# Layer norms of a two-layer backbone: the variance moved from VectorE's statistics operations to a squaring pass on ScalarE

## The chip, the cores and the metric

The kernel runs on one core of a Trainium2 chip. The metric is the device time of one execution in microseconds (us): the median of three runs of the kernel before is 2028.66 us, and its runs lie between 2025.94 and 2029.03 us. TensorE does matmuls and transposes, VectorE and ScalarE do elementwise work, GpSimd does a little elementwise work and starts some of the DMAs, and SyncE starts the weight DMAs.

## The reference, cut to what matters

Two layers of a backbone work on 384 tokens (128 context tokens and 256 latent ones) of width 1024. Each layer has three sub-layers (feed-forward, token mixer, feed-forward), and each ends in a layer norm of a weighted sum:

```python
def layer_norm(x, g, b):
    mu = jnp.mean(xf, -1, keepdims=True)
    var = jnp.mean(jnp.square(xf - mu), -1, keepdims=True)
    return ((xf - mu) * lax.rsqrt(var + LN_EPS) * g + b).astype(x.dtype)
...
    h = x * (1.0 + sc1) + sh1
    f = swiglu(h, lp['ffn_w_gate'][0], lp['ffn_w_up'][0], lp['ffn_w_down'][0])
    x = layer_norm(ALPHA * x + 0.5 * g1 * f, lp['ln_g'][0], lp['ln_b'][0])
```

So there are six norms in one execution. The output of a norm, modulated by a scale and a shift, is the input of the next sub-layer. The last norm gives the result.

## The kernel before, in words

The 384 tokens are three groups `g` of 128, one token per partition, in the tile `x[:, g, :]` (128 x 1024 float32). Norm `n` (0 to 5) stands behind sub-layer `n`. Norms 0 to 4 are worked in `turn_x(j)` of each engine's program, the lead-in of the next sub-layer, which has number `t = n + 1`, and `j = t % 3` (1: into a mixer; 0 or 2: into a feed-forward part); norm 5 is `norm_last`. Each engine runs its own instructions in program order, and the order across engines is made by semaphores alone, all written by hand. What an engine does for a group in a norm, in order of dependence:

- TensorE finishes the group's accumulation (`acc_done`).
- VectorE `residual(n, g)`, L2167: two products of 512 columns, from PSUM times the gate, into a residual tile. It frees the accumulation banks (`acc_read`).
- VectorE `rest(n, g)`, L2175: `x = ALPHA * x + residual` (L2178), two `bn_stats` of 512 columns (L2180), one `bn_aggr` that gives mean and variance (L2182, `stats_ready`).
- ScalarE `root(n, g)`, L1652: the square root of variance plus epsilon (L1654, `std_ready`).
- VectorE `scale(n, g)`, L2184: the reciprocal (L2186), and the mean times it, negated (L2187, `rstd_ready`).
- ScalarE `normalise(n, g)`, L1657: `x = x * rstd - mean * rstd` (L1659, `normed`).
- TensorE `turn_group(t, g)`, L826: eight transposes into two PSUM banks (`turned`).
- ScalarE `modulate`, L1664, on the first half and VectorE `modulate`, L2196, on the second half: scale and shift of the next sub-layer.
- ScalarE `high`, L1674: the rounded part of the modulated tile; VectorE `low`, L2206: the rest to it (`h_ready`). TensorE multiplies both, so its first product of the next sub-layer waits for `low` of group 0 and for the first half of `low` of group 1.

`weight(u)` is the same split of a unit of weights: ScalarE rounds it (L1650), VectorE takes the rest (L2161). The next sub-layer begins with groups 0 and 1 together in `tile_first` (L959), and takes group 2 behind them. In `turn_x` of VectorE for t of 2 and more (L2253 to L2276) the order is residual, rest and scale of group 0, the same of group 1, modulation of 0, residual of 2, weight 0, modulation of 1, the three `low` operations, weight 1, then rest and scale of group 2. ScalarE's order (L1713 to L1772) has the modulation of group 0 ahead of the root of group 1 for j of 2, and behind its normalisation for j of 0 and 1; for j of 0 two weights stand between normalisation 0 and root 1. For t of 1 VectorE takes all three groups one after the other (L2237), and ScalarE's queue has `ride_copy` and `ride_out` between them, copies of small products that SyncE's weight chunks and GpSimd's table of shifts (`ab_ready`) depend on. TensorE runs a few products without use (`keep_clock`, L837) while it waits.

In `norm_last` (L2329) VectorE does residual, rest and `finish` of one group after the other, and `finish` (L2332) applies gain and bias in two three-operand operations, in halves for the last group, whose stores follow.

## Time and profile before

| what | value |
|---|---|
| median of three runs | 2028.66 us (2025.94 to 2029.03) |
| span of the profiled execution | 2027.0 us |
| TensorE matmul busy | 1918.1 us, 95% |
| VectorE busy | 1042.7 us, 51% |
| ScalarE busy | 703.9 us, 35% |
| mean granted TensorE clock | 0.973 of full |

The span goes from the first to the last instruction of the profiled execution; it lies 1.66 us below the median of the timed runs and inside their range. A busy share is an average over stages. What a norm is worth is read from the stretch around it, by what each engine waits for there. In the rows, PE is TensorE, DVE is VectorE, ACT is ScalarE, L2180 is line 2180 of the kernel before, and a bracket at the end of a row gives the idle time in front of the instruction and what ended it.

### The profile page before, as it was taken

The numbers are of one execution on the slowest core, as the hardware profiler recorded it, in microseconds if no ns is written. First come the engines' busy times: TensorE is split into PE (matmuls) and PEld (weight loads), VectorE is DVE, ScalarE is ACT, GpSimd is POOL, SyncE is SP. The second block draws the span as 40 slices with busy tenths as digits, with TensorE's granted clock in tenths as the row PEclk, the third lists the DMA queues.
The fourth block names the chain that finished last, engine by engine and source line by source line (L and its number), as shares of the span: only waits on it lengthen the run. The fifth ranks groups of instructions, "written<-read, shape, count | busy, mean of one in ns | idle before, by whom it ended". The sixth has DMA issues, their size and how long they took to land.

```text
span 2027.0 us, 37395 instructions
## 1 busy us (share of the span) xinstructions
PE 1918.1 (95%) x16214; PEld 1731.7 (85%) x16214; DVE 1042.7 (51%) x1653; ACT 703.9 (35%) x1170; POOL 33.7 (2%) x69
## 2 busy tenths in 40 slices
PE   6999999998899899999999999999987989999996
PEld 5899997987679779999979999989766877899996
DVE  2333336555565775333364333466557768533336
ACT  3222224444442353222252222245364224322221
POOL 0000000000000001000000000000000000000000
PEclk8999999999989999999999999999998899899998
DMA  8733336333680145333344333323344004333330
GB/s 325 296 124 124 124 127 247 104 125 125 248 335 18 42 151 189 124 124 124 125 166 145 124 124 124 131 77 125 104 176 171 4 24 162 111 124 124 124 104 32
DMA packets 41473, 277.71 MB, mean 137 GB/s; under 512 B 4778, under 2 KB 6810, under 8 KB 9344
## 3 DMA queue, kind: packets, MB, share of 16 engines
q1 hardware_dynamic: 35424, 255.34, 34.9%
q0 software_dynamic: 3312, 16.91, 2.2%
q10 hardware_dynamic: 2608, 3.56, 0.5%
q8 instruction: 104, 1.70, 0.3%
q14 instruction: 25, 0.20, 0.0%
HBM read 269.22 MB, written 3.41 MB: 134 GB/s over the span
## 4 chain that ended last, share of the span: by engine, by line
PE 81%; DVE 11%; ACT 3%; issue 2%; DMA 1%; PEld 0%; ACTq 0%; PEldq 0%; SPq 0%; POOL 0%; DVEq 0%; POOLq 0%
PE bank L919 17%; PE bank L984 17%; PE bank L923 17%; PE bank L922 17%; PE bank L759 2%; PE bank L1372 1%; DMA ring<-weights 1%; PE bank L1361 1%; PE bank L1379 1%; DVE ring_r L2161 1%; DVE ln_stat L2180 1%; DVE x L2178 1%; PE bank L840 1%; PE bank L768 1%; DVE arena L2171 1%
## 5 line engine op out<-in xcount | busy, mean ns | idle before, releaser
L2161 DVE TENSOR_TENSOR ring_r<-ring,arena_r 128x1024 fp32r<-128x1024 f32 x328 | 387.7, 1221 | 706.5 <-ACT arena_r L1650 706.0
L919 PE MATMUL bank<-arena_r 128*128 128x384 f32 (+3 forms) x2056 | 700.8, 341 | 13.3 <-DVE arena_r L2210 11.2
L923 PE MATMUL bank<-arena_r,ring_r 128*128 128x384 f32 (+2 forms) x1816 | 604.9, 333 | 0.0
L922 PE MATMUL bank<-arena_r 128*128 128x384 f32 (+2 forms) x1816 | 602.9, 332 | 0.0
L919 PEld LDWEIGHTS bank<-arena_r 128*128 128x128 f32 x2056 | 391.5, 190 | 35.5 <-issue 20.0
L1650 ACT ACTIVATE arena_r<-ring 128x1024 fp32r<-128x1024 f32 x340 | 340.4, 1051 | 138.0 <-PE bank L923 136.6
L922 PEld LDWEIGHTS bank<-arena_r 128*128 128x128 f32 x1816 | 343.5, 189 | 3.5
L923 PEld LDWEIGHTS bank<-arena_r,ring_r 128*128 128x128 f32 x1816 | 343.6, 189 | 0.0
L984 PE MATMUL bank<-arena_r 128*128 128x512 f32 x1128 | 310.9, 393 | 0.3 <-issue 0.3
L1781 ACT ACTIVATE arena<-bank 128x384 f32<-128x384 f32 x88 | 43.3, 492 | 740.5 <-PE bank L923 740.5
L984 PEld LDWEIGHTS bank<-arena_r 128*128 128x128 f32 x1128 | 210.7, 188 | 42.2 <-issue 1.2
L984 PE MATMUL bank<-ring_r,arena_r 128*128 128x512 f32 x456 | 142.0, 392 | 0.0
L984 PEld LDWEIGHTS bank<-ring_r,arena_r 128*128 128x128 f32 x456 | 85.6, 188 | 19.8
L923 PE MATMUL bank<-arena_r 128*128 128x512 f32 (+1 forms) x240 | 89.7, 374 | 0.0
L922 PE MATMUL bank<-ring_r,arena_r 128*128 128x512 f32 (+1 forms) x240 | 89.4, 373 | 0.0
L759 PE MATMUL bank<-ring,silu_c 128*32 128x256 f32 x1152 | 73.6, 396 | 15.3 <-DMA const<-consts 9.6
L759 PEld LDWEIGHTS bank<-ring,silu_c 128*32 128x32 f32 x1152 | 34.8, 112 | 43.1 <-issue 18.9
L2297 DVE TENSOR_TENSOR arena<-arena,bank 128x384 f32<-128x384 f32 x88 | 48.2, 547 | 29.4 <-PE bank L923 29.4
L922 PEld LDWEIGHTS bank<-ring_r,arena_r 128*128 128x128 f32 x240 | 45.6, 190 | 9.6 <-issue 1.9
L923 PEld LDWEIGHTS bank<-arena_r 128*128 128x128 f32 x240 | 45.5, 189 | 8.5
L785 ACT ACTIVATE ride_row<-bank 112x512 f32<-112x512 f32 x36 | 21.4, 594 | 87.4 <-PE bank L759 87.3
L2301 DVE TENSOR_TENSOR arena_r<-arena,arena_r 128x384 fp32r<-128x384 f32 x88 | 49.2, 559 | 3.1
(295 smaller groups left out, 1817.6 us busy)
## 6 DMA issues: line engine op xcount, KB each, us to landing
ring<-weights SPq DMA_DIRECT2D x242, 1024.0 KB, 4.9
lnrow<-ln_in POOLq DMA_DIRECT2D x6, 1024.0 KB, 6.8
const<-consts POOLq DMA_DIRECT2D x1, 2211.0 KB, 9.5
arena<-gate POOLq DMA_DIRECT2D x4, 385.0 KB, 8.0
x<-x_in ACTq DMA_DIRECT2D x1, 1536.0 KB, 13.7
rows<-row_in POOLq DMA_DIRECT2D x2, 704.0 KB, 10.7
par<-par_in POOLq DMA_DIRECT2D x2, 662.5 KB, 7.5
y_out<-x SPq DMA_DIRECT2D x2, 512.0 KB, 2.6
```

The lines of the kernel that those rows point to most:

```text
L759: mm = pe.matmul(ps[bank][rows_at, half * 256:half * 256 + 256], silu_c[:, 2 * (k % 2):2 * (k % 2) + 32], ring_tile(n + half)[:, k, :], st ...
L768: mm = pe.matmul(ps[bank][:, at + 2 * i:at + 2 * i + 2], ride_row[:, number % 2, i * P:i * P + P], sel, start=True, stop=True)
L785: sc.activation(ride_row[0:RIDE_ROWS, number % 2, :], ps[bank][0:RIDE_ROWS, :], ACT.Copy).then_inc(ride_copied, 1)
L919: mm = pe.matmul(out, w_h, h_h, start=start, stop=False, skip_group_check=True)
L922: pe.matmul(out, w_h, h_l, start=False, stop=False, skip_group_check=True)
L923: return pe.matmul(out, w_l, h_h, start=False, stop=stop, skip_group_check=True)
L984: mm = pe.matmul(ps[2 + 2 * g + n][:, :], a[:, tok], w[:, n * 512:n * 512 + 512], start=(first and a is a_hi and w is hi), stop=(last and ...
L1650: sc.activation(place, unit_of((l, name), u), ACT.Copy).then_inc(w_rounded, 1)
L1781: sc.activation(sgt[:, b, :], ps[0][:, 0:TOK], ACT.Silu).then_inc(silu_done, 1)
L2161: ve.tensor_tensor(low_unit((l, name), u) if out is None else out, raw, place.bitcast(F32), ALU.subtract).then_inc(w_ready, 1)
L2297: ve.tensor_tensor(act[:, b, :], sgt[:, b, :], ps[1][:, 0:TOK], ALU.mult).then_inc(act_ready, 1)
L2301: ve.tensor_tensor(lo, act[:, b, :], hi.bitcast(F32), ALU.subtract).then_inc(act_split, 1)
```

## The change

The three statistics operations of `rest` go. The residual operation (L2178) gets an accumulator output, the row sum; one operation of one column turns it into the negated mean. `root` on ScalarE squares `x` minus the mean over all 1024 columns with a row sum, its output going to the spent residual tile, waits for it, and takes the root of the sum over 1024 plus epsilon. `scale` multiplies the negated mean by the reciprocal. VectorE's order in `turn_x` changes: `residual` of the next group stands ahead of `scale` of a group, `scale` of group 1 goes behind `modulate` of group 0, `rest` of group 2 goes ahead of the three `low` operations and its `scale` behind them, ahead of weight 1. The case t = 1 is written out in the same manner. ScalarE's order stays. In `norm_last` the product with the gain is taken before the root is there, into a tile of its own, and one operation (for the last group one of each half) is left behind the reciprocal.

```diff
--- before.py
+++ after.py
@@ -315,7 +315,6 @@
         ride_row = sb("ride_row", [P, 2, 512])
         gate = sb("gate", [P, 2, DM])
         lnrow, lnrow_r = with_rounded("lnrow", [P, 2, DM])
-        ln_stat = sb("ln_stat", [P, GROUPS, 12])
         small = sb("small", [P, 216])
         arena, arena_r = with_rounded("arena", [P, 23704])
 
@@ -528,7 +527,7 @@
         bonus = small[:, 136:160]
         gla_end_decay = small[:, 160:162]
         first_bias = small[:, 192:216]
-        ln_mv = small[:, 177:183].rearrange("p (g n) -> p g n", g=GROUPS)
+        ln_mean = small[:, 177:183].rearrange("p (g n) -> p g n", g=GROUPS)
         ln_r = small[:, 183:192].rearrange("p (g n) -> p g n", g=GROUPS)
         diff_gn = lnrow[:, 1, 0:P]
         eps_col = small[:, 176:177]
@@ -1650,8 +1649,11 @@
                         sc.activation(place, unit_of((l, name), u), ACT.Copy).then_inc(w_rounded, 1)
 
                     def root(n, g):
+                        spent = res_mix[:, g, :] if n % NMIX == 1 else res_ffn[:, g % 2, :]
                         sc.wait_ge(stats_ready, GROUPS * n + g + 1)
-                        sc.activation(ln_r[:, g, 0:1], ln_mv[:, g, 1:2], ACT.Sqrt,
+                        own.link(sc.activation(spent, x[:, g, :], ACT.Square, bias=ln_mean[:, g, 1:2],
+                                               accum_out=ln_r[:, g, 0:1]))
+                        sc.activation(ln_r[:, g, 0:1], ln_r[:, g, 0:1], ACT.Sqrt, scale=1.0 / DM,
                                       bias=eps_col[:, 0:1]).then_inc(std_ready, 1)
 
                     def normalise(n, g):
@@ -2175,21 +2177,16 @@
                     def rest(n, g):
                         res = res_of(n, g)
                         ve.wait_ge(acc_read, GROUPS * n + g + 1)
-                        own.link(ve.scalar_tensor_tensor(x[:, g, :], x[:, g, :], ALPHA, res, ALU.mult, ALU.add))
-                        for i in range(2):
-                            own.step(ve.bn_stats(ln_stat[:, g, 6 * i:6 * i + 6], x[:, g, i * 512:i * 512 + 512]))
-                        own.settle()
-                        ve.bn_aggr(ln_mv[:, g, :], ln_stat[:, g, :]).then_inc(stats_ready, 1)
+                        own.link(ve.scalar_tensor_tensor(x[:, g, :], x[:, g, :], ALPHA, res, ALU.mult, ALU.add,
+                                                         accum_out=ln_mean[:, g, 0:1]))
+                        ve.tensor_scalar(ln_mean[:, g, 1:2], ln_mean[:, g, 0:1], -1.0 / DM, None,
+                                         ALU.mult).then_inc(stats_ready, 1)
 
                     def scale(n, g):
                         ve.wait_ge(std_ready, GROUPS * n + g + 1)
                         own.link(ve.reciprocal(ln_r[:, g, 1:2], ln_r[:, g, 0:1]))
-                        ve.scalar_tensor_tensor(ln_r[:, g, 2:3], ln_mv[:, g, 0:1], -1.0, ln_r[:, g, 1:2], ALU.mult,
-                                                ALU.mult).then_inc(rstd_ready, 1)
-
-                    def statistics(n, g):
-                        residual(n, g)
-                        rest(n, g)
+                        ve.tensor_tensor(ln_r[:, g, 2:3], ln_mean[:, g, 1:2], ln_r[:, g, 1:2],
+                                         ALU.mult).then_inc(rstd_ready, 1)
 
                     LOWER, UPPER = slice(0, 4), slice(4, KT)
 
@@ -2235,9 +2232,15 @@
 
                         n = t - 1
                         if t == 1:
-                            for g in range(GROUPS):
-                                statistics(n, g)
-                                scale(n, g)
+                            residual(n, 0)
+                            rest(n, 0)
+                            residual(n, 1)
+                            scale(n, 0)
+                            rest(n, 1)
+                            residual(n, 2)
+                            scale(n, 1)
+                            rest(n, 2)
+                            scale(n, 2)
                             ve.wait_ge(ab_ready, t + 1)
                             modulate(j, 0)
                             modulate(j, 1)
@@ -2252,22 +2255,24 @@
                             return
                         if j == 1:
                             weight(0)
-                        statistics(n, 0)
+                        residual(n, 0)
+                        rest(n, 0)
+                        residual(n, 1)
                         scale(n, 0)
-                        statistics(n, 1)
-                        scale(n, 1)
+                        rest(n, 1)
                         ve.wait_ge(ab_ready, t + 1)
                         modulate(j, 0)
+                        scale(n, 1)
                         residual(n, 2)
                         if j != 1:
                             weight(0)
                         modulate(j, 1)
+                        rest(n, 2)
                         low(j, 0, 0)
                         low(j, 1, 1, LOWER)
                         low(j, 2, 1, UPPER)
+                        scale(n, 2)
                         weight(1)
-                        rest(n, 2)
-                        scale(n, 2)
                         if j != 1:
                             for u in range(2, 4):
                                 weight(u)
@@ -2328,15 +2333,17 @@
 
                     def norm_last():
                         n = NMIX * DEPTH - 1
+                        gained = arena[:, 0:GROUPS * DM].rearrange("p (g n) -> p g n", g=GROUPS)
 
                         def finish(g):
 
+                            ve.wait_ge(stats_ready, GROUPS * n + g + 1)
+                            own.step(ve.scalar_tensor_tensor(gained[:, g, :], x[:, g, :], ln_mean[:, g, 1:2], lnrow[:, 0, :],
+                                                             ALU.add, ALU.mult))
                             ve.wait_ge(std_ready, GROUPS * n + g + 1)
                             own.link(ve.reciprocal(ln_r[:, g, 1:2], ln_r[:, g, 0:1]))
                             for c in (slice(0, 512), slice(512, DM)) if g == GROUPS - 1 else (slice(0, DM),):
-                                own.link(ve.scalar_tensor_tensor(x[:, g, c], x[:, g, c], ln_mv[:, g, 0:1], lnrow[:, 0, c],
-                                                                 ALU.subtract, ALU.mult))
-                                ve.scalar_tensor_tensor(x[:, g, c], x[:, g, c], ln_r[:, g, 1:2], lnrow[:, 1, c], ALU.mult,
+                                ve.scalar_tensor_tensor(x[:, g, c], gained[:, g, c], ln_r[:, g, 1:2], lnrow[:, 1, c], ALU.mult,
                                                         ALU.add).then_inc(x_ready, 1)
 
                         ve.wait_ge(lnrow_loaded, 16 * NMIX * DEPTH)
```

## Rows read from the trace of the kernel before

**Rows 1.** the page: the span, and the chain that ended last by engine

```profile
span 2027.0 us, 37395 instructions
...
PE 81%; DVE 11%; ACT 3%; issue 2%; DMA 1%; PEld 0%; ACTq 0%; PEldq 0%; SPq 0%; POOL 0%; DVEq 0%; POOLq 0%
```

**Rows 2.** instructions by line and shape, VectorE; columns: count | busy us, mean ns | idle before

```profile
L2180 DVE BATCH_NORM_STATS2 ln_stat<-x 128x6 f32<-128x512 f32 x36 | 23.2, 685 | 0.6
...
L2178 DVE SCALAR_TENSOR_TENSOR x<-x,arena 128x1024 f32<-128x1024 f32 x18 | 22.0, 1223 | 0.5
...
L2182 DVE BATCH_NORM_AGGREGATE small<-ln_stat 128x2 f32<-128x12 f32 x18 | 3.8, 209 | 0.6
```

**Rows 3.** the same view, ScalarE: normalisation, root, its table load, read-out of a row sum

```profile
L1659 ACT ACTIVATE x<-x,small 128x1024 f32<-128x1024 f32 x15 | 18.7, 1244 | 6.4 <-DVE small L2187 6.4
...
L1654 ACT ACTIVATE small<-small 128x1 f32<-128x1 f32 x18 | 5.3, 294 | 79.3 <-DVE small L2182 79.3
...
L1654 ACT ACT_TABLE_LOAD x4 | 5.1, 1283 | 0.1
...
L1926 ACT ACTIVATION_READ_ACCUMULATOR wad<-arena 128x1 f32 x24 | 4.8, 201 | 0.0
```

**Rows 4.** timeline of ScalarE in layer 0's mixer; columns: start us, us, line, operation

```profile
698.41 1.49 ACT L2103 ACTIVATE arena<-arena 128x1536 f32<-128x1536 f32 x1 [1.48 <-DVE arena L2784]
...
702.45 1.28 ACT L2110 ACT_TABLE_LOAD   x1
```

**Rows 5.** the chain that ended last, final norm; columns: start us, us, what

```profile
2009.87 1.21 DVE arena L2171 x2
...
2017.06 1.21 DVE arena L2171 x2
...
2023.88 0.75 DVE x L2339
```

**Rows 6.** timeline, norm 1 (behind layer 0's mixer): up to the first products

```profile
735.54 1.50 ACT L1670 ACTIVATE arena<-bank,ab 128x128 f32<-128x128 f32 x4
...
740.10 1.06 PE L834 MATMUL bank<-const,x 128*128 128x128 f32 x8 [0.29 <-issue]
...
741.67 1.36 DVE L2202 TENSOR_SCALAR arena<-bank,ab 128x128 f32<-128x128 f32 x4
...
742.95 2.42 DVE L2210 TENSOR_TENSOR arena_r<-arena,arena_r 128x1024 fp32r<-128x1024 f32 x3
...
744.91 0.36 PE L919 MATMUL bank<-arena_r 128*128 128x256 f32 x1 [1.51 <-DVE arena_r L2210]
```

**Rows 7.** timeline, norm 1: the third group of 128 tokens

```profile
754.45 1.36 DVE L2202 TENSOR_SCALAR arena<-bank,ab 128x128 f32<-128x128 f32 x4
...
756.55 0.30 PE L919 MATMUL bank<-arena_r 128*128 128x128 f32 x1 [1.38 <-DVE arena_r L2210]
```

**Rows 8.** timeline, norm 2 (behind layer 0's second feed-forward part)

```profile
1028.25 1.99 ACT L1650 ACTIVATE arena_r<-ring 128x1024 fp32r<-128x1024 f32 x2
...
1033.38 1.06 PE L834 MATMUL bank<-const,x 128*128 128x128 f32 x8 [0.29 <-ACT x L1659]
...
1039.03 0.36 PE L919 MATMUL bank<-arena_r 128*128 128x256 f32 x1 [1.65 <-DVE arena_r L2210]
```

**Rows 9.** timeline, norm 3 (behind layer 1's first feed-forward part)

```profile
1328.70 1.96 PE L903 MATMUL bank<-arena,wad 128*64 128x128 f32 x16 [2.01 <-ACT arena L1670]
...
1333.02 2.42 DVE L2210 TENSOR_TENSOR arena_r<-arena,arena_r 128x1024 fp32r<-128x1024 f32 x3
...
1341.41 1.06 PE L834 MATMUL bank<-const,x 128*128 128x128 f32 x8 [0.29 <-ACT x L1659]
```

**Rows 10.** timeline, norm 0: root of the third group

```profile
338.97 0.28 ACT L1654 ACTIVATE small<-small 128x1 f32<-128x1 f32 x1
```

**Rows 11.** stretches: length, busy us (instructions) of each engine, granted clock, DMA share, GB/s

```profile
1325.00:1350.00 25.00, 20.94 (x162) 19.53 (x161) 14.22 (x36) 11.32 (x22) 0.00 (x0) 0.93 0.00 1
1720.00:1760.00 40.00, 38.25 (x208) 35.22 (x209) 24.32 (x33) 15.47 (x24) 0.54 (x1) 0.87 0.32 120
```

## The prediction

> **What bounds the kernel now.** I read the page first: the chain that ended last is TensorE for 81% of the span and VectorE for 11% [rows 1]. So inside a sub-layer VectorE and ScalarE cost nothing, and a norm counts only where TensorE waits for it. Then I went through the timeline around each of the six norms, looking on TensorE's rows for a bracket. At norms 0 to 4 TensorE stands before the first product of the next sub-layer (1.51 and 1.65 us at norms 1 and 2 [rows 6, 8]) and again before the third group (1.38 us [rows 7]). Behind norm 5 no matmul is left: the chain is VectorE alone, 7.19 us from one group to the next (2009.87 to 2017.06), and 7.57 us from there to the last operation's end (2023.88 + 0.75) [rows 5]. In the lead-in of norm 1 VectorE is busy without a break from 741.67 to the first product; in that of norm 2 ScalarE's queue carries the start (two weights at 1028.25, the normalisation, then transposes at 1033.38) [rows 6, 8].
>
> **The change, one group alone.** Removed from VectorE: two statistics of 0.685 us and one closing operation of 0.209; back to back with their gaps they fill 1.56 us of the path. Kept: the residual operation, 1.223 us [rows 2]. Added on VectorE: the read of the row sum and an operation of one column. No VectorE row shows an accumulator output; the nearest is ScalarE's read, 0.201 us [rows 3]. It may hide wholly, so I bound it by 0 and 0.20 and take 0.10, between. The one-column operation is bounded by the closing operation it resembles, 0.21 [rows 2], and I take 0.20 with its gap. Added on ScalarE: the square over 1024 columns. With two column operands such an ACTIVATE takes 1.244 [rows 3], with none about 1.0 (1.99 for two [rows 8]); it has one, so 1.15, and its read adds 0.10 of its 0.20 behind it (bounds 0 and 0.20). New path: 0.30 + 0.03 + 1.25 = 1.58 against 1.56. **The latency of one group doesn't change.** VectorE gets 1.26 us free, ScalarE gets 1.25 more. The change is worth something only where VectorE is the bound and has other work meanwhile.
>
> **The table load.** The root needs ScalarE's table to be changed behind each feed-forward part: four loads of 1.283 us, with 0.1 us of idle in front of all four together [rows 3]. Today they are issued while the engine would wait for statistics (79.3 us of waiting ahead of the 18 roots [rows 3]), at no cost. In the mixer a square stands ahead of a root: the square at 698.41 has no load in front of it, the load comes at 702.45, directly ahead of the root [rows 4]. I take it that the same happens here: the square runs under the old table and the load comes between square and root. It then lies on the first group's path at norms 0, 2, 3 and 5, at 1.28 us each.
>
> The Trainium skill's page "ScalarE: Activation LUTs", section "Table sets: the hidden batching unit", says that cheap functions are in every set as filler and that the load is placed right before the activation whose function is not in the active set. By that rule, which speaks against this change, the load comes behind the square; the mixer's rows agree for one set, and no row here shows a square under the feed-forward part's set. If it were not there, the third rival below holds.
>
> **Norm 5** (nothing hides it). Group 0: latency 1.56 is traded for 1.58, the gain product (1.28) runs beside the square, and the load adds 1.28: 0.0. Group 1: the gain product leaves the path: 7.19 - 1.28 = 5.9, -1.3. Group 2: the two halves' gain products leave, 1.5: -1.5. Sum -2.8, bounds -3.1 and -2.3 by the reads.
>
> **Norms 1 and 4** (behind a mixer, twice the same). ScalarE modulates group 0 from 735.54 for 1.50 [rows 6], to 737.04, and only then comes to root 1, although VectorE's sum for group 1 is ready some 2.5 us sooner than the statistics were. Square and read 1.25, root 0.29 [rows 3], VectorE's two small operations 0.36, normalisation 1.24 [rows 3], less one overlap: 740.2, and the transposes start at 740.35 instead of 740.10 [rows 6]. Their second half is there 1.1 later, at 741.45; VectorE modulates 1.36, to 742.8, a little ahead of before (741.67 + 1.36 [rows 6]). But now `rest` of group 2 stands ahead of the three `low` operations: 1.22 + 0.30 = 1.53, to 744.35. From the start of the `low` operations to the first product were 744.91 - 742.95 = 1.96 [rows 6]: first product at 746.3, +1.4. At the third group VectorE's modulation began at 754.45 only when weights 2 and 3 were done [rows 7]; group 2's root is now earlier and they will be out of the way. ScalarE's half limits that: -0.5, bounds 0 and -1.0, inside the 1.38 of waiting there [rows 7]. **+0.9 each.** Weight 1 now waits behind `scale` of group 2, and so behind a square; it comes just in time for the second early product (2.9 us behind the first); if not, up to +0.4.
>
> **Norm 2.** VectorE's latency being equal, ScalarE is later by the load: its two weights end at 1028.25 + 1.28 + 1.99 = 1031.5 [rows 8]. Square and read 1.25, root 0.29, small operations 0.40, normalisation 1.24: 1034.7, transposes from 1033.38 to 1034.95, +1.6 [rows 8]. Second half 1.1 later, modulation 1.36, `rest` of group 2 1.53, 1.96 to the first product: 1040.9 instead of 1039.03 [rows 8], +1.9. Weight 1 is late here by 0.3, the third group gives back 0.5: **+1.7**.
>
> **Norm 3.** TensorE is still at work on the last tiles, which hides the load. But `scale` of group 1 now waits behind `modulate` of group 0, and the square is on ScalarE: modulation 0 and the first `features` product (1328.70 with 2.01 of waiting [rows 9]) come 1.2 later. The `low` operations, at 1333.02 before [rows 9], come 1.2 + 1.53 later. Before, TensorE took the first product at about 1335.2, 0.2 behind them because of its own work; so +2.5. The third group's transposes at 1341.41 waited 0.29 for a normalisation [rows 9], which is early now: **+2.2**.
>
> **Norm 0.** The root of group 2 at 338.97 [rows 10] stands on the path by ScalarE's queue: its statistics were long there. Behind it are the copies that the table of shifts waits for. So the square is added whole, 1.25, and the scale of group 1, now behind the residual of group 2, delays a copy by up to 0.4. **+1.6.**
>
> **Sum:** 1.6 + 0.9 + 1.7 + 2.2 + 0.9 - 2.8 = +4.5. Against the profiled span that is 2027.0 + 4.5 = 2031.5; that execution's span lies 1.66 below the median of the runs, so 2033.2. A tile inside a feed-forward part is bound by TensorE, so what is lost ahead of it isn't regained. What a measurement can tell from no change is about 0.2%, 4.1 us: the bounds are 2024.6 and 2032.7.
>
> **Rivals.**
> 1. A further clock fall. In the lead-in of norm 4 the granted clock falls: 0.87 over 40 us [rows 11], so 0.13 x 2 x 40 = 10.4 us at the lower level, 1.2 instead of 2.4 GHz, which costs half of it, 5.2. Norms 1 and 2 have nearly the same waits and their rows no fall. The change makes TensorE's wait ahead of norm 1's first product 2.7 instead of 1.5. One more such fall: 2033.2 + 5 = 2038.
> 2. The other side, not slower: the clock is regained. If the wait at the third group, shorter by 0.5, no longer ends in a fall at norm 4, -5.2; the smaller fall at norm 3 (0.93 over 25 us [rows 11], 3.5 us at the lower level) gives 1.8 at most. It decides from one fall gone: 2028.0; with both, 2026.2; with both and the lead-ins half as dear, 2023. Against it: other waits grow.
> 3. The load goes ahead of the square, hidden as before: -1.3 at norm 5 and -1.3 at norm 2, none at norms 0 and 3: 2030.6.
> 4. The lead-ins are hidden and only norm 5 counts: 2028.7 - 2.8 = 2025.9; with the load hidden too, 2024.6. For it: 1.26 us less of VectorE per group where VectorE is the bound. Against it: ScalarE's order, and the place of `rest` of group 2.
> 5. The change doesn't do what it says (the sum is not kept by the operation and the pass is rebuilt): within 0.2%.
>
> **How the numbers follow.** Forecast 0.38, of it 0.31 slower and 0.07 same (its own range, 2031 to 2035.5, crosses the bound); rival 1 0.18, slower; rival 2 0.21, 0.13 same and 0.08 faster; rival 3 0.08, same; rival 4 0.12, 0.08 same and 0.04 faster; rival 5 0.03, same. Slower 0.49, same 0.39, faster 0.12. The likeliest is the forecast, 2033.2. Range 2025.5 to 2038.5: it takes in rivals 3 and 5, most of 1, 2 and 4, and leaves out some 0.08 below and 0.08 above.
>
> **What would show it.** Per group: the row sum ready 1.55 us behind the residual product, a square of 1.15. A table load between the first square and root of norms 0, 2, 3 and 5; if it stands ahead of the square, that step is wrong. First product behind the transposes: 1.4 later at norm 1, with the sum operation of group 2 between VectorE's modulation and `low`. The end: 5.9 us from group 1 to group 2. The prediction is wrong if the accumulator costs far more than 0.2 on VectorE, if the lead-ins don't lengthen, or if stretches at the lower clock appear or vanish.

## The result: 0.59% slower, and the profile after

| | before | changed |
|---|---|---|
| median of 7 runs | 2028.66 us | 2037.03 us |
| lowest and highest | 2020.76 to 2032.96 | 2035.55 to 2039.71 |
| profiled execution, span | 2027.0 | 2033.4 |

The ratio of the two kernels is 1.0059, with a 95% interval of 1.0042 to 1.0076: 12 us slower, between 8.5 and 15.4. (It isn't the quotient of the medians, which lie 8.4 us apart.) The sign was forecast, the size was not: +4.5 lies below the whole interval. The page of the changed kernel, span and chain that ended last (before: [rows 1]):

```profile
span 2033.4 us, 37412 instructions
...
PE 84%; DVE 8%; ACT 4%; issue 2%; DMA 1%; PEld 0%; ACTq 0%; PEldq 0%; SPq 0%; DVEq 0%; POOL 0%; POOLq 0%
```

VectorE's share of the chain fell from 11 to 8%, ScalarE's rose from 3 to 4%, and TensorE's rose from 81 to 84%, although it has the same matmuls to do. That last figure is the trail to follow.

Instructions of the changed kernel by line and shape (line, engine, operation, count | busy us, mean ns | idle before); they answer to [rows 2, 3]:

```profile
L2180 DVE SCALAR_TENSOR_TENSOR x<-x,arena 128x1024 f32<-128x1024 f32 x18 | 22.0, 1221 | 0.3
...
L1654 ACT ACTIVATE arena<-x,small 128x1024 f32<-128x1024 f32 x18 | 20.7, 1148 | 48.9 <-DVE small L2182 48.9
...
L1661 ACT ACTIVATE x<-x,small 128x1024 f32<-128x1024 f32 x15 | 18.6, 1242 | 13.6 <-DVE small L2188 13.6
...
L1656 ACT ACT_TABLE_LOAD x4 | 5.1, 1283 | 0.1
...
L1654 ACT ACTIVATION_READ_ACCUMULATOR arena<-x,small 128x1 f32 x18 | 3.4, 190 | 0.0
```

The square takes 1.148 us where 1.15 was taken. The residual operation, now with a row sum, takes the 1.22 us it took without one.

**Norm 5**, the chain that ended last in the changed kernel (start us, us, what); it answers to [rows 5], to which this row of the kernel before, the start of its group 0, belongs:

```profile
2002.59 1.30 DVE arena L2171 x2
```

The changed kernel:

```profile
2012.08 1.30 DVE arena L2173 x2
...
2014.68 0.16 DVE small L2182
...
2014.87 1.24 ACT arena L1654 x2
...
2016.13 1.28 ACT L1656
...
2019.23 1.21 DVE arena L2173 x2
...
2025.01 1.21 DVE arena L2173 x2
...
2029.49 0.75 DVE x L2346
2030.24 0.66 DVEq L802
```

From group 0 to group 1 it takes 7.15 us (7.28 before), from group 1 to group 2 5.78 (7.19 before), and from there to the end of the last operation 5.89 (7.57 before). The load of 1.28 us lies on the path at 2016.13, behind the square. Norm 5 got 3.2 us shorter.

**Norm 1**, timeline of the changed kernel (start us, us, engine, line, operation, in brackets the wait ahead and who ended it); it answers to [rows 6]:

```profile
743.55 1.07 PE L833 MATMUL bank<-const,x 128*128 128x128 f32 x8 [0.50 <-ACT x L1661]
...
744.65 1.37 DVE L2199 TENSOR_SCALAR arena<-bank,ab 128x128 f32<-128x128 f32 x4 [0.20 <-PE bank L833]
...
745.94 1.22 DVE L2180 SCALAR_TENSOR_TENSOR x<-x,arena 128x1024 f32<-128x1024 f32 x1
...
747.08 0.08 DVE L2180 DVE_READ_ACCUMULATOR x<-x,arena 128x1 f32 x1
...
747.27 2.42 DVE L2207 TENSOR_TENSOR arena_r<-arena,arena_r 128x1024 fp32r<-128x1024 f32 x3
...
749.23 0.35 PE L918 MATMUL bank<-arena_r 128*128 128x256 f32 x1 [2.38 <-DVE arena_r L2207]
```

Group 2's sum stands between modulation and `low`, as forecast, and costs 1.33 (745.94 to 747.27). Modulation follows the transposes in 1.10 instead of 1.57 (741.67 - 740.10 [rows 6]); before, VectorE was at the rest of a weight until then, and now it is free sooner. The read of the row sum takes 0.08 us and the residual operation ends under it.

**Norm 2**, timeline of ScalarE in the changed kernel:

```profile
1031.43 1.15 ACT L1654 ACTIVATE arena<-x,small 128x1024 f32<-128x1024 f32 x1 [9.70 <-DVE small L2182]
1032.49 0.18 ACT L1654 ACTIVATION_READ_ACCUMULATOR arena<-x,small 128x1 f32 x1
1032.69 1.28 ACT L1656 ACT_TABLE_LOAD   x1
1033.98 0.29 ACT L1656 ACTIVATE small<-small 128x1 f32<-128x1 f32 x1
```

The square runs under the table of the feed-forward part, and the load comes behind it, directly ahead of the root.

**The clock.** A fall, below, is a stretch in which the granted clock is the lower of its two levels, 1.2 instead of 2.4 GHz. Stretches over the lead-ins of norms 0, 1, 2, 3 and 4 in the changed kernel (length, busy us of each engine, granted clock, DMA share, GB/s), and then over norms 0, 1 and 2 in the kernel before:

```profile
330.00:365.00 35.00, 32.01 (x272) 28.00 (x271) 14.64 (x36) 18.29 (x38) 1.14 (x5) 0.95 0.48 191
735.00:765.00 30.00, 25.44 (x203) 20.14 (x202) 18.07 (x37) 21.57 (x37) 0.00 (x0) 0.94 0.45 176
1028.00:1064.00 36.00, 31.59 (x229) 25.32 (x228) 21.15 (x42) 24.66 (x40) 0.00 (x0) 0.95 0.47 176
1310.00:1355.00 45.00, 40.53 (x246) 37.44 (x245) 23.46 (x44) 20.91 (x31) 0.00 (x0) 0.96 0.27 94
1715.00:1760.00 45.00, 40.45 (x289) 34.33 (x288) 29.99 (x52) 28.44 (x46) 0.00 (x0) 0.96 0.39 152
```

```profile
325.00:362.00 37.00, 34.52 (x318) 29.19 (x316) 20.70 (x44) 17.18 (x35) 1.14 (x5) 1.00 0.57 233
730.00:760.00 30.00, 25.95 (x213) 20.31 (x212) 23.35 (x43) 19.01 (x32) 0.00 (x0) 1.00 0.46 176
1022.00:1055.00 33.00, 29.52 (x226) 23.31 (x225) 24.91 (x45) 19.78 (x33) 0.00 (x0) 1.00 0.49 192
```

Each of the five lead-ins now has one short stretch of 3.4 us at 1.2 GHz (0.05 x 2 x 35 = 3.5), where before norms 0, 1 and 2 had none. In exchange the longer fall at norm 4 (0.87 over 40 us [rows 11]) is gone from this execution.

**The feed-forward parts.** Nothing in the change touches them, and still each takes longer at full clock. In the chain that ended last the down products of a tile appear once per tile, as one row. (A feed-forward part is the stretch of a feed-forward sub-layer between two lead-ins; there are four, 0 to 3.) The 1st and the 16th of these rows in part 0, kernel before, then changed kernel:

```profile
105.52 4.17 PE bank L984 x18
...
294.28 4.15 PE bank L984 x18
```

```profile
105.75 4.17 PE bank L983 x18
...
295.25 4.17 PE bank L983 x18
```

15 tiles in 188.76 us against 189.50: a tile takes 12.584 us before and 12.633 after. There are 88 tiles, so some 4 us. No step of the prediction has this.

To see what each stretch costs, I set the matmuls of two traces beside each other one for one (the small ones that keep the clock left out) and took the time between the same two. Where no fall of the clock lies in a feed-forward part, these times repeat from one execution to the next within some 0.05 us. "low" is the time at 1.2 GHz, "from" the start of the stretch in the kernel before:

| stretch, us | from | before | changed |
|---|---|---|---|
| start | 0 | 87.52 (low 10.2) | 87.65 (low 10.2) |
| ffn part 0 | 87.52 | 238.53 | 239.50 |
| norm 0 lead-in | 326.05 | 34.75 | 37.18 (low 3.4) |
| mixer 0 | 360.79 | 368.44 (low 30.7) | 368.23 (low 23.9) |
| norm 1 lead-in | 729.23 | 29.12 | 31.15 (low 3.4) |
| ffn part 1 | 758.36 | 250.43 | 251.44 |
| norm 2 lead-in | 1008.79 | 44.15 | 46.62 (low 3.4) |
| ffn part 2 | 1052.94 | 243.68 | 244.63 |
| norm 3 lead-in | 1296.61 | 52.98 (low 3.4) | 54.86 (low 3.4) |
| mixer 1 | 1349.60 | 333.67 (low 41.0) | 332.97 (low 34.1) |
| norm 4 lead-in | 1683.27 | 55.34 (low 5.4) | 55.09 (low 3.4) |
| ffn part 3 | 1738.61 | 258.54 (low 4.9) | 257.33 |
| norm 5 and end | 1997.15 | 29.89 | 26.71 |

### The profile page after: what moved, and what is told of

Its sections match the earlier page's. It is cut to its first block, busy times and chain, and to the rows that moved or that the text cites. A ratio compares the mean times of both kernels' runs of the same rounds, so it can differ in the third digit from the quotient of the medians.

```text
span 2033.4 us, 37412 instructions
## 1 busy us (share of the span) xinstructions
PE 1921.4 (94%) x16214; PEld 1731.9 (85%) x16214; DVE 1019.6 (50%) x1634; ACT 724.3 (36%) x1206; POOL 33.7 (2%) x69
## 4 chain that ended last, share of the span: by engine, by line
PE 84%; DVE 8%; ACT 4%; issue 2%; DMA 1%; PEld 0%; ACTq 0%; PEldq 0%; SPq 0%; DVEq 0%; POOL 0%; POOLq 0%
PE bank L918 18%; PE bank L921 17%; PE bank L922 17%; PE bank L983 17%; PE bank L758 2%; PE bank L1371 1%; DMA ring<-weights 1%; PE bank L1360 1%; PE bank L1378 1%; PE bank L839 1%; PE bank L767 1%; ACT arena L1672 1%; PE bank L833 1%; DVE x L2180 1%; ACT arena L1654 1%
```

## Experiments

Two theories stood at the start. **Place**: the change takes away a tile (`ln_stat`, 144 bytes of each partition), so `small` and the `arena`, which holds TensorE's operands, lie 144 bytes lower, and the matmuls run at another pitch. **Norms**: the lead-ins cost more than forecast, by themselves or by falls of the clock. Each series of timed kernels below was run beside the kernel before on one chip; its median there was 2025 to 2027 us. A mean clock or a time is of all timed executions of a kernel; stretches are of the one that was profiled. "Tiles in place" means the changed kernel with the unused tile of the second experiment.

### The kernel before again

No edit.

> The kernel before once more, profiled on the chip of the next three. It is the yardstick for two things: the pitch of the matmuls inside the feed-forward loops and the stretches at the lower TensorE clock. If the pitch belongs to the kernel, matmuls 600 to 1600 of TensorE take 190.5 us here as in the first profile (191.3 in the changed kernel). If it belongs to the chip or the execution, it is anything between. Ratio to itself 1.000.

Measured: ratio 0.9995 (0.9982 to 1.0009). So a difference under 0.2% says nothing here.

### Changed kernel, tiles back in place

```diff
+        spacer = sb("spacer", [P, GROUPS, 12])
         small = sb("small", [P, 216])
```

> The changed kernel with a tile of 144 bytes per partition put back where the statistics tile was, so that all later tiles lie where they lay before. Theory P (the place of the tiles sets the matmuls' pitch): the drift inside the four feed-forward parts, some 0.8 to 1.1 us in each and about 4 us in all, goes: about 4 us faster than the changed kernel, ratio to the kernel before 1.004. Theory Q (pitch is of the chip or execution): no difference to the changed kernel, ratio 1.006.

Measured: 2031.63 us, ratio 1.0021 (1.0007 to 1.0036). The feed-forward parts are 238.56, 250.44, 243.68 and 256.29 us, those of the kernel before (256.27 for the last, in an execution without a fall there). By the two ratios an unused tile takes back more than half of the loss.

### Kernel before, tiles moved

```diff
-        ln_stat = sb("ln_stat", [P, GROUPS, 12])
         small = sb("small", [P, 216])
         arena, arena_r = with_rounded("arena", [P, 23704])
+        ln_stat = sb("ln_stat", [P, GROUPS, 12])
```

> The kernel before with the same statistics tile allocated behind the large one, so that the large one and the small one lie 144 bytes lower, as in the changed kernel; no instruction differs. Theory P: about 4 us slower, ratio 1.002. Theory Q: ratio 1.000.

Measured: 2035.22 us, ratio 1.0054 (1.0034 to 1.0075), with not one instruction changed. Its chain that ended last, the same two tiles as above:

```profile
105.59 4.17 PE bank L984 x18
...
295.09 4.17 PE bank L984 x18
```

189.50 us, exactly the changed kernel's. So place alone makes a slower kernel, and the norms alone do not explain the result. Every product of a tile is made of three lines of matmuls (high by high, high by low, low by high). In part 0 the matmuls of 384 columns of the first line stand 175.9 ns ahead of the next one in the kernel before, and 179.4 here (means of 298); the two other lines move by 1.1 at most.

### Table load ahead of the wait

Edit on top of the changed kernel with its tiles in place:

```diff
+                        if g == 0 and n % NMIX != 1:
+                            sc.activation(table_col, eps_col, ACT.Sqrt)
                         sc.wait_ge(stats_ready, GROUPS * n + g + 1)
```

> The padded changed kernel with one more root of a single column ahead of the wait for group 0's sum at norms 0, 2, 3 and 5, so that the table load comes there. Forecast's step: 1.3 us less at norm 5 and 1.3 at norm 2, none at norms 0 and 3, so 2.6 us under e2. Rival (the load is covered by other work): no difference to e2.

Measured: ratio 1.0028 (1.0014 to 1.0042); the same, within the intervals, as without the edit. Norm 5 took 25.42 us instead of 26.68, the whole load. But norm 2's lead-in gained 0.3 only (45.19 instead of 45.46 at full clock). Timeline of norm 2 in this kernel, ScalarE and VectorE:

```profile
1031.78 0.30 ACT L1659 ACTIVATE small<-small 128x1 f32<-128x1 f32 x1
1031.81 1.29 DVE L2176 TENSOR_TENSOR arena<-bank,gate 128x512 f32<-128x512 f32 x2 [1.34 <-PE bank L984]
1033.01 0.15 DVE L2190 RECIPROCAL small<-small 128x1 f32<-128x1 f32 x1
...
1033.40 1.25 ACT L1664 ACTIVATE x<-x,small 128x1024 f32<-128x1024 f32 x1 [1.32 <-DVE small L2191]
```

The root ends at 1032.08, but its reciprocal stands behind the residual product of group 1, which VectorE took up at 1031.81, and ScalarE waits 1.32 us. What the early load gives, the new order on VectorE takes. So at norm 2 the load was not the price; order and load cover each other.

### Group 2's sum back in its old place

Edit on top of the changed kernel with its tiles in place: `rest(n, 2)` and `scale(n, 2)` behind the `low` operations and `weight(1)`, as before.

```diff
                         modulate(j, 1)
-                        rest(n, 2)
                         low(j, 0, 0)
...
+                        weight(1)
+                        rest(n, 2)
                         scale(n, 2)
-                        weight(1)
```

> The padded changed kernel with the sum operation of group 2 and its scale put back behind the three low operations and weight 1. The forecast's step: 1.5 us less ahead of the first product at norms 1, 2 and 4 and up to 2 at norm 3, so 5 us under e2, and the 0.5 us at the third group lost again where the weights 2 and 3 are late. Rival (ScalarE's queue is the bound, not this operation): under 1 us.

Measured: ratio 1.0039 (1.0020 to 1.0057), no gain. Norm 1 in this kernel:

```profile
745.35 1.37 DVE L2200 TENSOR_SCALAR arena<-bank,ab 128x128 f32<-128x128 f32 x4 [0.20 <-PE bank L834]
746.63 2.42 DVE L2208 TENSOR_TENSOR arena_r<-arena,arena_r 128x1024 fp32r<-128x1024 f32 x3
748.60 0.36 PE L919 MATMUL bank<-arena_r 128*128 128x256 f32 x1 [1.05 <-DVE arena_r L2208]
```

From modulation to first product it is 3.25 us instead of 4.58 (744.65 to 749.23), the 1.33 of the sum, as forecast. But then the third group is late by 1.0 of it, and the lead-in as a whole gains 0.34 (29.31 against 29.65). At norm 2 it gains nothing (45.44 against 45.46): VectorE still waits 1.31 us there for ScalarE's high parts, ahead of the second `low`, so the sum had cover. Norm 3 gains 0.9 (53.97 against 54.86, each with a fall of 3.4 us).

### New form at norm 5 alone

Norms 0 to 4 stay with `bn_stats` and their old order; norm 5 takes the new sum, square and `finish`, with the table load ahead of its wait; `ln_stat` stays, so the tiles are in place.

```diff
-                            root(n, g)
+                            square_root(n, g)
...
-                            rest(n, g)
+                            summed(n, g)
```

> The kernel before at norms 0 to 4, with the changed form at norm 5 alone and the table load ahead of the wait; all tiles lie where they lay before. Forecast's step: 4.1 us faster than before (0.0 + 1.3 for the load at group 0, 1.3, 1.5), ratio 0.998, with no change at any lead-in.

Measured: 2021.06 us, ratio 0.9979 (0.9961 to 0.9997). Norm 5 takes 25.43 us instead of 29.89, and nothing else moves. Again in a later series:

> The kernel with the new form at the last norm alone and the table load ahead of its wait, with its tiles as before, once more beside the others of this series: ratio 0.998 (2021 us where the kernel before takes 2025.5), which is the 4.5 us by which its last norm is shorter. The label's name notwithstanding, its arena is where it was before. It bounds how far a repeat of five rounds moves, and says whether the last norm's gain holds in a second series.

Measured: 2022.80 us, ratio 0.9978 (0.9964 to 0.9992). The 4.5 us hold.

### More matmuls to keep the clock

Edit on top of the changed kernel with its tiles in place:

```diff
-WARM_START, WARM_MIX, WARM_TURN, WARM_GLA = 22, 6, (3, 6, 10), (7, 10)
+WARM_START, WARM_MIX, WARM_TURN, WARM_GLA = 22, 10, (7, 8, 14), (7, 10)
```

> The padded changed kernel with four more products without use in each wait of TensorE at norms 1 to 4 (0.25 us each; two at norm 3's second wait). If the longer waits bring the short falls of the clock (one of 3.4 us in each lead-in of the changed kernel's profile, 1.7 us each), they go at norms 1 to 4 and up to 6 us come back; if the falls come at any rate, nothing does or up to 1 us is lost.

Measured: 2027.58 us, ratio 1.0007 (0.9991 to 1.0023), against 1.0021 (1.0007 to 1.0036) without the edit; the intervals overlap. The mean clock of the timed runs is 0.9796, against 0.9763. The profiled execution has one short fall, at norm 0, and two of 10 us in parts 1 and 2. That count alone says little: the kernel with group 2's sum back in its old place, without the added matmuls, has no short fall at norms 0, 1, 2 and 4.

Several executions with tiles in place give each lead-in at full clock (us): norm 0 36.18 (from the kernel with its tiles in place and the one with group 2's sum back in its place), norm 1 29.64, norm 2 45.46, norm 3 53.15, norm 4 53.65 (from this one). The kernel before has 34.75, 29.12, 44.15, 51.2 and 53.14; 51.2 is from kernels with the arena moved, which read 51.2 to 51.4, and 53.14 from the kernel with the new form at norm 5 alone.

### Changed kernel again, beside the others

No edit.

> The changed kernel unaltered, timed beside the kernel before in the same series as the others. If the place of the tiles costs what the shifted kernel before showed (some 1.0 us in each feed-forward part, about 4.4 us in all), this run lies about 4 to 6 us above the changed kernel with its tiles put back: ratio 1.004 to 1.006, with feed-forward parts at 239.5, 251.4, 244.6 and 257.3 us. If the place costs nothing in timed runs, the ratio is the 1.002 of the kernel with its tiles put back, and the rest of the 1.006 measured first belonged to that series.

Measured: 2037.15 us, ratio 1.0060 (1.0039 to 1.0081), with parts of 239.51, 251.43, 244.58 and 257.32 us. The 1.006 belongs to the kernel, not to its first series.

### Which bytes, and by what rule

Five places of the kernel before. The first was timed, the others were profiled once each. 4 unused bytes ahead of the arena (`spacer`, [P, 1]):

> The kernel before with the large tile moved up by 4 bytes, so that its start, 4 bytes short of a multiple of 64 bytes before and 20 bytes short in the changed kernel, is a multiple of 64. No instruction differs. If the pitch goes by how far operands lie from such a multiple, the 1.0 us per feed-forward part that 144 bytes down cost come with another sign or size: up to 16 ns of each product of 384 columns (175 ns now, 160 at 2.4 GHz), 80 us in all, at the most. If only a conflict between two tiles counts (distances inside the large tile don't change), the pitch stays as before: ratio 1.000.

Measured: ratio 1.0030 (1.0009 to 1.0051). 64 bytes ahead of it ([P, 16]):

> The kernel before with an unused tile of 64 bytes ahead of the operand arena: arena starts 64 bytes higher, its start modulo 64 stays 60. If the start modulo 64 sets the pitch of the feed-forward matmuls, the four parts take what they take before, 238.5, 250.4, 243.7 and 256.3 us. If it goes by another property of the address (modulo 128 or more, or the distance to another tile), they move by up to 1.0 us each. Timed runs are not asked for: without falls of the clock these parts repeat to 0.02 us.

16 bytes ([P, 4]):

> The kernel before with an unused tile of 16 bytes ahead of the arena: start modulo 64 is 12 in place of 60. If the pitch goes by the start modulo 64, the parts lie anywhere between 238.5 and 239.5 us for the first and move together, as with the 4 bytes (239.0). If only the distance to the small tiles below counts, they stay at 238.5.

`ln_stat` behind the arena and 16 bytes ahead of it, so the arena lies 128 bytes lower:

> The kernel before with the norm statistics' tile behind the arena and 16 bytes unused ahead of the arena: the small tiles lie 144 bytes lower, as in the changed kernel, the arena 128 bytes lower and so at its old start modulo 64. If the arena's start modulo 64 sets the pitch, the feed-forward parts are those of the kernel before (238.5, 250.4, 243.7, 256.3 us). If the place of the small tiles does, they are those of the changed kernel (239.5, 251.4, 244.6, 257.3 us).

And `ln_stat` behind the arena with 144 bytes ahead of it, so that only `small` is moved:

> The kernel before with the norm statistics' tile behind the arena and 144 unused bytes ahead of the arena: only the small tiles are moved, the arena starts at its old place. If the place of the arena alone sets the pitch of the matmuls, all parts are those of the kernel before: 238.5, 250.4, 243.7, 256.3 us. If the small tiles have a part in it, or the distance between the two, they differ by 0.3 us or more each.

Measured, feed-forward parts without falls of the clock, us (a dash where one lay in the part; the row of -144 is the changed kernel's, and parts 0, 1 and 3 of the moved one agree within 0.02). The last two columns are the heads of the mixers, between the same two matmuls in every trace (360.79 to 476.07 and 1349.60 to 1462.48 in the kernel before), where no execution has a fall:

| arena moved by | small moved by | part 0 | part 1 | part 2 | part 3 | mixer 0, head | mixer 1, head |
|---|---|---|---|---|---|---|---|
| 0 | 0 | 238.5 | 250.4 | 243.7 | 256.3 | 115.3 | 112.9 |
| 0 | -144 | 238.6 | 250.4 | 243.7 | - | 115.3 | 112.9 |
| -144 | -144 | 239.5 | 251.4 | 244.6 | 257.3 | 115.3 or 115.7 | 112.9 or 114.2 |
| +4 | 0 | 239.0 | 251.0 | 244.2 | 256.8 | 116.3 | 113.9 |
| +16 | 0 | 239.0 | 251.0 | 244.2 | - | 116.3 | 113.9 |
| +64 | 0 | 238.2 | - | 243.4 | 255.9 | 117.1 | 114.7 |
| -128 | -144 | 236.4 | 248.2 | 241.4 | 253.9 | 116.2 | 113.7 |

Of the two tiles it is the arena's place that counts: with only `small` moved nothing changes. And my rule fell: +64 and -128 leave the start modulo 64 as it was, and the first moves part 0 by 0.3 us and the second by 2.2.

The heads of the mixers move as well, and not by the same rule as the parts: +1.7 us in all at -128, where the parts are shortest, +2.0 at +4 and +16, and +3.7 at +64, more than the parts give back there. At -144 the place doesn't settle them: the changed kernel's first profiled execution has the heads of the kernel before, its second one and that of the moved kernel have 1.7 us more. So the place at -128 is worth -9.0 + 1.7 = -7.3 us, and the one at -144 +4.0 or +5.7. The tile's time at -128, from the chain of that kernel:

```profile
104.81 4.12 PE bank L985 x18
...
291.81 4.12 PE bank L985 x18
```

187.00 us for 15 tiles, 12.467 each, and every row of down products 0.03 to 0.05 shorter. In part 0 there, the three lines of matmuls stand 173.9, 173.5 and 174.0 ns ahead of the next one, steadily from the seventh matmul of a tile on. In the kernel before, the gaps go round in a pattern of nine matmuls, whose longest is 178 to 179 in one tile and 185 in the next; at -144 they go round in a pattern of six with one of 185 in every tile. So what differs is a rhythm in the starts of the matmuls. By what rule the place sets it stays open.

### Do place and norms add up?

The kernel before and the changed kernel, both with the arena 128 bytes lower, timed:

> The same kernel as the last one, timed. Its parts without falls of the clock sum to 9 us less than before: 2017 to 2019 us, ratio 0.995 to 0.997 to the kernel before. If that execution was an odd one, 1.000.

> The changed kernel with 16 unused bytes ahead of the arena, so that its tiles lie as in the last kernel (small tiles 144 bytes lower than before, arena 128 bytes lower). If the place of the tiles and the layer norms are two separate terms, the feed-forward parts are those of that kernel (236.4, 248.2, 241.4, 253.9 us), the layer norms those of the changed kernel, and the time lies some 13 us below the changed kernel and 3 to 7 us above the kernel before with the same tiles. If the short feed-forward parts came from something else in that one execution, they come back to 238 to 240 us.

Measured: 2021.41 us, ratio 0.9979 (0.9961 to 0.9996), and 2023.11 us, ratio 0.9984 (0.9968 to 1.0000). The changed kernel's parts are 236.4, 248.1, 241.4 and 253.9 us, its lead-ins those it has elsewhere. One unused tile of 16 bytes makes the changed kernel 14 us faster (2037.15 to 2023.11, in two series), and no slower than the kernel before.

The kernel before gained less in its timed runs (4 to 5 us) than its four parts give (9.0), and the moved kernel lost more (11) than its parts give (4.0). 1.7 us of either is in the heads of the mixers. And both had the clock against them: a mean of 0.9751 and 0.9739 against 0.9775 of the kernel before. Over all timed executions, 136 of the kernel before and 140 of the others, a span fell by 0.9 us for each 0.001 of mean clock. Compared at one mean clock of 0.977, the spans stand to the kernel before, beside what the stretches at full clock give (parts, heads of the mixers and norms):

| kernel | difference by timed runs, us | by stretches, us |
|---|---|---|
| changed (two series) | +10.4 and +11.1, each ± 2 | +6.4 or +8.1 |
| changed, tiles in place | +4.5 ± 1.5 | +2.4 |
| before, arena at -144 | +6.7 ± 1.8 | +5.7 |
| before, arena at +4 | +5.1 ± 1.6 | +4.1 |
| before, arena at -128 | -6.5 ± 1.6 | -7.3 |
| changed, arena at -128 | -2.9 ± 1.6 | -4.9 |
| norm 5 alone (two series) | -4.3 and -3.3, each ± 1.5 | -4.5 |

Norms: +4.5, +3.6 (-2.9 + 6.5) and +4.1 (10.75 - 6.7). Place: +6.7 and +6.3 (10.75 - 4.5) at -144; -6.5 and -7.4 (-2.9 - 4.5) at -128. The two add up. The place's terms agree with the stretches; the norms' are some 2 us above them. The other kernels with the new norms and tiles in place stand at +4.4 (table load ahead), +5.6 (group 2's sum back) and +3.8 (more matmuls): none is clear of the +4.5.

### The two good parts together

Norm 5 alone, and the arena at -128:

> The kernel before with the new form at the last norm alone, the table load ahead of its wait, and its tiles placed as in the two kernels whose feed-forward parts are 2.2 us shorter (arena 128 bytes lower). If place and last norm add up, its parts are 236.4, 248.2, 241.4, 253.9 us and 25.4 us behind the last accumulation, and it takes 2013 to 2017 us, ratio 0.993 to 0.996. If the gain of the place in timed runs is eaten by falls of the clock, as part of it was without the new form, 0.996 to 0.998.

Measured: 2015.96 us, ratio 0.9947 (0.9927 to 0.9966), faster than both kernels; its span at one clock is 10.7 ± 1.8 below the kernel before (by stretches -7.3 - 4.5 = -11.8). With more matmuls that keep the clock as well:

> The kernel of the run before it with more of the small matmuls that keep TensorE busy in the waits of the lead-ins (10 in place of 6; 7, 8, 14 in place of 3, 6, 10). If the falls of the clock behind the layer norms are the remaining loss, its mean granted clock rises by some 0.002 to 0.003 as it did with the changed kernel, and it gains a further 2 to 3 us: ratio 0.992 to 0.994. If in this kernel the falls stand elsewhere (the mixers), nothing, or a loss of up to 2 us where the added matmuls delay the third group.

Measured: 2015.04 us, ratio 0.9949 (0.9931 to 0.9967), the same; mean clock 0.9766 against 0.9771. In the profiled execution of each, about 10 us at 1.2 GHz lie on norm 2 and the part behind it, with and without the added matmuls. Here they had nothing to win.

## Why the prediction was wrong

**The step that failed is the sum, which has no term for the place of the tiles.** The deletion of `ln_stat` stands in the diff, and I read it as a line without cost. It moves the arena by 144 bytes, and every feed-forward tile takes 0.05 us longer: +4.0 us by the parts, in two of three profiled executions another 1.7 in the mixers, and +6.3 to 6.7 by timed runs at one clock. Shown both ways, by adding it to the kernel before and by taking it from the changed one. "What is lost ahead of a feed-forward part isn't regained" was right, "a tile inside is bound by TensorE" too; that its pace could change was not thought of.

Point by point, at full clock:

- **One group's latency.** Forecast 1.58 against 1.56. Measured 1.45: 0.16 for the small operation, 1.24 for square and read, and gaps. The sum's read hides under the residual operation but for 0.01 (I took 0.10), the read of ScalarE behind the square but for 0.09.
- **The load** lies between square and root at norms 0, 2, 3 and 5, as forecast. "ScalarE: Activation LUTs" of the Trainium skill, section "Table sets: the hidden batching unit", says that a load is put before every activation that needs one; the trace agrees, with no load ahead of the square at 1031.43 and one ahead of the root at 1032.69. Rival 3 fell. Its price of 1.28 is right at norm 5 and wrong at norm 2, where only 0.3 of it comes back without it.
- **Norm 5.** Forecast -2.8, measured -3.2: -0.13, -1.41 and -1.68 for 0.0, -1.3 and -1.5, by the shorter latency three times.
- **Norms 1 and 4.** Forecast +0.9 each, measured +0.5: first product +1.0 instead of +1.4 (VectorE's modulation follows the transposes sooner), third group -0.46 for -0.5.
- **Norm 2.** Forecast +1.7, measured +1.3. Turn of group 1 +1.3 instead of +1.6, first product +1.4 instead of +1.9, because `rest` of group 2 had cover; the third group gave back 0.1 and not 0.5.
- **Norm 3.** Forecast +2.2, measured +1.9: features +1.1 for +1.2, first product +2.3 for +2.5. **Norm 0**: +1.6 and +1.4.
- **Sum at full clock**: 1.4 + 0.5 + 1.3 + 1.9 + 0.5 - 3.2 = **+2.4** for +4.5. Each term had its sign right; the lead-ins were forecast 1.7 us too dear, and norm 5 gains 0.4 more than forecast.
- **Rival 1** (a further fall) came in another form: not one of 5 us, but 3.4 us at 1.2 GHz in each of norms 0, 1, 2 and 4, which cost 1.0, 1.5, 1.2 and 1.4 us, 5.1 in all. **Rival 2** came as well: norm 4's longer fall is gone, -4.5 (55.34 - 53.15 and 258.54 - 256.28). I had them as alternatives; the trace shows both at once, and that they nearly cancel there is chance. The short ones are more frequent with the change: norms 0, 1, 2 and 4 have 4, 4, 4, 3, 2, 1 and 0 of them in seven profiled executions with the new norms, 18 in all; in thirteen with the old norms 0 to 4 there are 4, all at norm 2. The long ones come and go: about 10 us at the lower clock across a lead-in and its feed-forward part is there in 9 of those 13 executions, and in 2 of the 7. They were no ground for a forecast from one execution.
- **Rivals 4 and 5** fell: the lead-ins are not hidden, and the time left the 0.2%.

The two profiled executions differ by 6.3 us, and the ledger closes: +2.4 norms, +4.0 place, +5.1 short falls, -4.5 the long one, +0.15 start, -0.9 mixers (both with several falls) is +6.3. The timed difference of 12 us (8.5 to 15.4) is larger. The profiled execution of the kernel before has a span of 2027.0, and the mean of its timed spans in the later series is 2023.8; the changed kernel's is 2033.4, and 2034.7 in the mean of both series: 4.5 us of the gap are that the first profile lies 3.2 above the mean of its kernel and the second 1.3 below its own. Another 0.55 lies outside the span (2.78 us against 2.23). At one mean clock 10.4 and 11.1 are measured, each ± 2, and 2.4 + 4.0 are located in the lead-ins and parts; the heads of the mixers give 1.7 more in the changed kernel's second profile, and none in its first. What stays open is 2 to 4 us, near the width of the interval. Some 2 of them go with the norms: the kernels with the new norms lie that much above their stretches at each of the three places of the arena, those with the place alone within 1. Where they lie no run here separates.

## What to carry to other kernels

A line that only frees a tile is an edit like any other: see which tiles behind it move, and run the change once with an unused tile in its place, or half of what is measured may be read as the algorithm's. The place of TensorE's operands was worth -7.3 to +5.7 us here by the stretches (-6.5 to +6.7 by timed runs), more than the change. Moving a row's statistics from VectorE to ScalarE pays where VectorE is alone on the path and has other work (norm 5: -4.5 us with the table loaded ahead) and costs where ScalarE's queue carries the next stage; take it norm by norm.

## What the runs showed of the hardware

- The same matmuls on operands 4 to 144 bytes apart in on-chip memory run at tile times of 12.467 to 12.633 us, 1.3% from best to worst, and repeat within 0.05 us in a part of 240. The best place for the feed-forward tiles isn't the best for the mixers: at -128 bytes the parts are 9.0 us shorter and the heads of the mixers 1.7 longer.
- At the head of a mixer one and the same kernel ran at two paces: 115.29 and 112.88 us in one execution of the changed kernel, 115.69 and 114.16 in another, without a fall of the clock in either.
- A row sum at VectorE's residual operation costs 0.08 us for its read, and nearly none of it on the path: 1.25 with it, 1.24 without. ScalarE's read behind a square takes 0.19 and adds 0.09.
- A short fall of the granted clock (3.4 us) in a lead-in costs 1.0 to 1.5 us, less than half its length, though TensorE's rows show it busy throughout. At norm 1 its matmuls of 256 columns go from 0.12 to 0.21 us apart, less than double; at norm 2 1.5 us are lost and 0.3 of them come back at the third group.
